# Top-k selection rounds moved from their own stage into VectorE's attention program

## The reference, cut to what matters

```python
def dsa_attention(q, k, v, iq, ik, iw, table):
    topk = min(TOPK_MAX, S // 4)                       # 128
    def block(args):                                   # one block of 128 queries
        logits = jnp.einsum('bqhd,bkd->bqhk', iqb, ik) * (IDX_DIM ** -0.5)
        score = jnp.einsum('bqhk,bqh->bqk', jax.nn.relu(logits), iwb)
        score = jnp.where(kpos <= qpos, score, NEG)
        _, idx = lax.top_k(score, topk)
        ...                                            # softmax over the 128 chosen keys alone
```

```python
        s = jnp.where(dist >= 0, s + bias[None, :, None], NEG)
        p = jax.nn.softmax(s, axis=-1)
        attn = p[:, :, 0] - lam * p[:, :, 1]
        return jnp.einsum('bhqk,bkhd->bqhd', attn, v32)
```

## Time and profile before

| | us |
|---|---|
| median of 3 runs (3939.85 to 3941.1) | 3940.17 |
| the profiled execution | 3943.98 |
| its span | 3942.2 |
| selection stage: first matmul to VectorE's last end | 3120.0 to 3187.9 |
| attention stage: first matmul to the last copy's end | 3189.5 to 3303.8 |

### The profile page before, as it was taken

The page is one execution under the profiler, slowest core; times in us unless marked ns, Lnnn a source line. Parts: engine busy times, 40 slices in busy tenths (PEclk is TensorE's granted clock), DMA queues, the critical chain, the costliest instruction groups (busy, mean ns, idle before and its releaser), DMA issues. The chain is left out here.

```text
span 3942.2 us, 48730 instructions
## 1 busy us (share of the span) xinstructions
PE 3447.4 (87%) x20802; PEld 2819.7 (72%) x20802; DVE 2049.6 (52%) x2787; ACT 1211.1 (31%) x1716; POOL 0.2 (0%) x4
## 2 busy tenths in 40 slices
PE   7999953688999999999944769999999957999998
PEld 6888842577688888888832668788888634868886
DVE  5444348646454445344357555453454487536565
ACT  3223222114332233223132024332232335434343
POOL 0000000000000000000000000000000000000000
PEclk9999977669999999999976569999999868999999
DMA  3322210003223222232200003122222110412222
GB/s 124 102 91 97 96 48 5 1 2 123 70 95 103 91 97 96 97 100 93 96 27 5 2 20 133 58 97 96 96 96 96 49 72 30 133 54 95 95 97 79
DMA packets 78095, 301.65 MB, mean 77 GB/s; under 512 B 8854, under 2 KB 9494, under 8 KB 77240
## 3 DMA queue, kind: packets, MB, share of 16 engines
q1 hardware_dynamic: 77880, 298.53, 22.4%
HBM read 292.47 MB, written 6.03 MB: 76 GB/s over the span
## 5 line engine op out<-in xcount | busy, mean ns | idle before, releaser
L307 DVE TENSOR_TENSOR w_lo<-ring,w_hi 128x1024 fp32r<-128x1024 f32 (+1 forms) x508 | 652.5, 1286 | 533.3 <-ACT w_hi L300 533.2
L319 PE MATMUL ps<-xa_hi,w_hi 128*128 128x512 f32 x1728 | 682.4, 395 | 83.9 <-DVE w_lo L307 82.4
L300 ACT ACTIVATE w_hi<-ring 128x1024 fp32r<-128x1024 f32 (+1 forms) x508 | 555.7, 1099 | 547.9 <-DMA ring<-in_mix_in_dram 203.0
L320 PE MATMUL ps<-xa_lo,w_hi 128*128 128x512 f32 x1728 | 676.6, 392 | 0.0
L321 PE MATMUL ps<-xa_hi,w_lo 128*128 128x512 f32 x1728 | 676.2, 391 | 0.0
L319 PE MATMUL ps<-xb_hi,w_hi 128*128 128x512 f32 x1248 | 487.9, 391 | 0.0
L321 PE MATMUL ps<-xb_hi,w_lo 128*128 128x512 f32 x1248 | 485.6, 389 | 0.0
L320 PE MATMUL ps<-xb_lo,w_hi 128*128 128x512 f32 x1248 | 485.6, 389 | 0.0
L319 PEld LDWEIGHTS ps<-xa_hi,w_hi 128*128 128x128 f32 x1728 | 326.5, 189 | 161.1 <-DVE w_lo L307 85.0
L320 PEld LDWEIGHTS ps<-xa_lo,w_hi 128*128 128x128 f32 x1728 | 327.0, 189 | 68.7 <-issue 1.9
L321 PEld LDWEIGHTS ps<-xa_hi,w_lo 128*128 128x128 f32 x1728 | 326.9, 189 | 68.5
(11 more groups left out here) (341 smaller groups left out, 3795.4 us busy)
## 6 DMA issues: line engine op xcount, KB each, us to landing
ring<-in_ffn_in_dram SPq DMA_DIRECT2D x176, 512.0 KB, 3.2
ring<-in_ffn_out_dram SPq DMA_DIRECT2D x64, 704.0 KB, 4.0
ring<-in_mix_in_dram SPq DMA_DIRECT2D x58, 512.0 KB, 3.2
ring<-in_up_dram SPq DMA_DIRECT2D x44, 512.0 KB, 3.2
ring<-in_w_in_dram SPq DMA_DIRECT2D x22, 512.0 KB, 3.2
ring<-in_down_dram SPq DMA_DIRECT2D x16, 704.0 KB, 4.1
ring<-in_mix_out_dram SPq DMA_DIRECT2D x16, 512.0 KB, 3.2
ring<-in_xk_dram SPq DMA_DIRECT2D x16, 512.0 KB, 3.3
```

What stands on the lines that cost most here:

```text
L300: act.activation(core.w_hi[j][:, 0:width], core.ring[j][:, 0:width], ACT.Copy).then_inc(self.halved, 1)
L307: dve.tensor_tensor(core.w_lo[j][:, 0:width], core.ring[j][:, 0:width], core.w_hi[j][:, 0:width].bitcast(F32), ALU.subtract).then_inc(self ...
L319: pe.matmul(out, hi, x_hi, start=(k == 0), stop=False)
L320: pe.matmul(out, hi, x_lo, start=False, stop=False)
```

## The change

The 16 rounds and the three last `tensor_scalar` leave the selection stage. In the attention stage VectorE runs one round (`choose(n)`) behind each of the units n = 0 to 15, and the three `tensor_scalar` behind unit 16. They now work in place, in `work`, which lies where `unpicked` lay. The sparse heads wait for them by a semaphore `chosen`.

```diff
-def select_keys_and_bias(core, rel_bias, reach_rows, reach_flags, skewed):
+def score_keys_and_bias(core, rel_bias, reach_rows, reach_flags, skewed):
...
-    work = core.scr[:, 5, :].rearrange("p (n k) -> p n k", n=3)
+    work = core.scr[:, 4, :].rearrange("p (n k) -> p n k", n=3)
...
-    unpicked = core.scr[:, 4, :].rearrange("p (n k) -> p n k", n=3)
-    best = core.small[:, 0:24].rearrange("p (n k) -> p n k", n=3)
...
-            maxed, out = [maxed0, maxed1, maxed2], [out0, out1, out2]
-            for n in range(TOPK // 8):
-                for i in range(1, QT):
-                    if n:
-                        dve.wait_ge(out[i - 1], n)
-                    dve.max(best[:, i - 1, :], work[:, i - 1, 0:(i + 1) * P]).then_inc(maxed[i - 1], 1)
-                for i in range(1, QT):
-                    row = work[:, i - 1, 0:(i + 1) * P]
-                    dve.wait_ge(maxed[i - 1], n + 1)
-                    dve.match_replace(row, best[:, i - 1, :], row, TAKEN).then_inc(out[i - 1], 1)
-            for i in range(1, QT):
-                dve.wait_ge(out[i - 1], TOPK // 8)
-                link(dve.tensor_scalar(unpicked[:, i - 1, 0:(i + 1) * P], work[:, i - 1, 0:(i + 1) * P], -2e38, NEG,
-                                       ALU.is_ge, ALU.mult))
...
@@ def block2_attention(core):
+    work = core.scr[:, 4, :].rearrange("p (n k) -> p n k", n=3)
+    best = core.small[:, 66:90].rearrange("p (n k) -> p n k", n=3)
...
                     if h >= 8 and i:
...
-                        dve.tensor_tensor(s, s, unpicked[:, i - 1, 0:width], ALU.add).then_inc(picked, 1)
+                        dve.wait_ge(chosen, 3)
+                        dve.tensor_tensor(s, s, work[:, i - 1, 0:width], ALU.add).then_inc(picked, 1)
...
+            maxed, out = [maxed0, maxed1, maxed2], [out0, out1, out2]
+
+            def choose(n):
+
+                for i in range(1, QT):
+                    if n:
+                        dve.wait_ge(out[i - 1], n)
+                    dve.max(best[:, i - 1, :], work[:, i - 1, 0:(i + 1) * P]).then_inc(maxed[i - 1], 1)
+                for i in range(1, QT):
+                    row = work[:, i - 1, 0:(i + 1) * P]
+                    dve.wait_ge(maxed[i - 1], n + 1)
+                    dve.match_replace(row, best[:, i - 1, :], row, TAKEN).then_inc(out[i - 1], 1)
...
             for n in range(len(units)):
                 turn_of(n + 2, n)
+                if n < TOPK // 8:
+                    choose(n)
+                if n == TOPK // 8:
+                    for i in range(1, QT):
+                        row = work[:, i - 1, 0:(i + 1) * P]
+                        dve.wait_ge(out[i - 1], n)
+                        dve.tensor_scalar(row, row, -2e38, NEG, ALU.is_ge, ALU.mult).then_inc(chosen, 1)
```

More of the change, by code:

```diff
@@ L1991, in select_keys_and_bias @@
     spread = core.spare[:, 0:HEADS * REACH].rearrange("p (h x) -> p h x", h=HEADS)
-    work = core.scr[:, 5, :].rearrange("p (n k) -> p n k", n=3)
+    work = core.scr[:, 4, :].rearrange("p (n k) -> p n k", n=3)
     part = core.scr[:, 6, 0:2 * S].rearrange("p (n k) -> p n k", n=2)
-    unpicked = core.scr[:, 4, :].rearrange("p (n k) -> p n k", n=3)
-    best = core.small[:, 0:24].rearrange("p (n k) -> p n k", n=3)
     n_parts = 3 * IDX
-    with stage(nc, "scored", "clipped", "added", "step", "maxed0", "maxed1", "maxed2", "out0", "out1", "out2",
+    with stage(nc, "scored", "clipped", "added", "step",
                "rows_in", "table_in", "flags_in", "made", "copied", "kept", "shifted") as (
-            block, scored, clipped, added, step, maxed0, maxed1, maxed2, out0, out1, out2,
+            block, scored, clipped, added, step,
             rows_in, table_in, flags_in, made, copied, kept, shifted):
@@ L2109, in block2_attention @@
     with stage(nc, "scored", "biased", "topped", "exped", "inverted", "shared", "turned", "turned_out", "gathered",
-               "stored", "weighted", "picked") as (
+               "stored", "weighted", "picked", "maxed0", "maxed1", "maxed2", "out0", "out1", "out2", "chosen") as (
             block, scored, biased, topped, exped, inverted, shared, turned, turned_out, gathered, stored,
-            weighted, picked):
+            weighted, picked, maxed0, maxed1, maxed2, out0, out1, out2, chosen):
         @block.tensor
@@ L2460, in block2 @@
     block2_small(core)
-    select_keys_and_bias(core, io["rel_bias"], io["reach"], io["flags"], skewed)
+    score_keys_and_bias(core, io["rel_bias"], io["reach"], io["flags"], skewed)
     block2_attention(core)
```

## The result

| kernel | median, us | runs, us | ratio to before, 95% interval |
|---|---|---|---|
| before, first comparison | 3940.64 | 3939.85 to 3943.39, n = 4 | |
| changed, first comparison | 4018.67 | 4016.93 to 4020.99, n = 4 | 1.0197 [1.0179, 1.0215] |
| changed, second comparison (29 runs of before) | 4019.27 | 4017.65 to 4023.47, n = 6 | 1.0123 [1.0071, 1.0175] |

The change costs 78 us in the first comparison, where 35.6 were forecast. The second ratio is smaller because the kernel before has two groups of times, which only the longer series of the experiments showed. In the three series behind the experiments 49 of its 89 runs took 3940 to 3949 us (the lower group) and 40 took 3981 to 3987 (the upper group), with nothing between. The runs that stand ahead of the prediction all fell in the lower group. All ten runs of the changed kernel lie at 4017 to 4023.

A forecast was written before the change was run, and what follows sets the result against it. VectorE was taken to bound heads 0 to 3, TensorE heads 4 to 11. Terms -6.1 + 44.4 - 1.7 - 1.0 + 0 = +35.6 us on 3940.2 gave 3975.8 us, range for 8 in 10 3967 to 3987.

The forecast's parts named there:

- What bounds what: Attention stage: VectorE bounds heads 0 to 3, TensorE bounds heads 4 to 11.
- The selection stage: Without the rounds, the bias read-back comes last, landing 11.0 us after issue; the stage gets 6.1 us shorter.
- Price and number of the rounds: Heads 0 to 3: rounds 0 to 14 are on the path, 15 x 2.96 = +44.4 us.
- the waits: Among the two-map units, VectorE's four waits for scores go: -1.7 us.
- round 15: Behind unit 15's combine: this round and the closing passes cost 0, barely covered by TensorE's work at 1.2 GHz.
- The backlog's -1.0: At unit 15: TensorE's backlog goes, so the transposes follow the combine some 0.1 us later: -1.0 us.
- TensorE's clock: Heads 4 and 5: low level again taken for 15 us, each microsecond at 1.2 GHz costing 0.40; its duration couldn't be read.
- rival 3: Heads 4 to 11: the clock stays low through all these single-map heads, +34 us, time 4010; chance 8%.
- Rival 1: Behind unit 15: the clock rises as soon as TensorE is dense, -3.6 us, time 3972; chance 20%.

The follow-up runs named there:

- e10: The changed kernel again, unaltered, beside more runs of before: 4017.65 to 4023.47 us, six of six.
- e3: Changed kernel with three added 128x128x512 matmuls in each of turns 15 and 16: 3981.4 to 3986.8 us, median 3983.5.
- e7: Kernel before with three added 128x128x512 matmuls in each of turns 15 and 16: 3941.1 to 3952.6 us, median 3949.3, ratio 0.9949.
- e1: Changed kernel with the 16 rounds left out of both stages: seven runs at 3933.2 to 3938.5 us, three at 3977.9 to 3982.3.
- e5: Changed kernel with rounds 0 to 7 in the selection stage, others behind units 0 to 7: four runs 3954.0 to 3958.5 us, six 3998.7 to 4002.9.
- e6: Changed kernel with rounds 0 to 7 in the selection stage, the others behind units 8 to 15: ten runs, 3983.6 to 4000.4 us.
- e9: Kernel before with one added matmul in each fourth unit of heads 4 to 11, eight in all: 3945.5 to 3959.9 us, median 3954.8.
- e2: Changed kernel with two added matmuls in each of turns 0 to 15: 3974.5, 3979.2, 4019.0 and 4019.5 us.
- e4: Changed kernel with rounds 0 to 13 back in the selection stage, 14 and 15 behind units 18 and 22, closing passes behind 23: median 3977.3 us.
- e8: As e4, with three added matmuls in each of turns 15 and 16: 3971.2 to 3983.0 us, median 3978.5.
- e12: Kernel before with two added matmuls in turns 1, 5, 9, 13 and one in 12, 14, 15: median 3940.8 us, ratio 0.9932.
- e13: As e12, plus two matmuls in turn 16, round 15 behind unit 15, closing passes behind 16: median 3937.6 us, ratio 0.9931 to before.

## Why the prediction was wrong

- **What bounds what** was right: VectorE in heads 0 to 3 (80.00 of 80 us busy in after, no wait for scores), TensorE in heads 4 to 11.
- **The selection stage** gave 6.9 us for the 6.1 forecast: the read-back landed in 10.7 for 11.0, and the way to it was a little shorter as well. In the second profile of the changed kernel (e10) it landed in 11.1, so this much varies from run to run.
- **Price and number of the rounds**: 42.0 us to the combine of unit 15 for 42.7 forecast, the waits were won back, and the transpose of unit 16 (3276.52) did not wait for round 15 at the low clock. The backlog's -1.0 came out too: unit 15's transposes follow its combine by 0.06 us, where it took 1.15 in before.
- **The sum of these** is confirmed a second way. Between the groups that can be compared, the changed kernel's 4019.0 is 35.7 us above before's upper group (median 3983.2), and e3 is 34.1 above e7, for 35.6 forecast.
- **The step that failed is TensorE's clock**: "How long the low level then lasts is what I can't read, and I take 15 us again." It lasted over all eight heads, which the prediction had as rival 3 at 8% and +34 us; measured +35.7 in the stretch behind unit 15, where -1.0 was forecast. The error was twofold. The prediction took the 15 us as a property of the heads, where it is one draw of a spread: 40 of 89 runs of the kernel before are 42 us slower. No profile of before fell on one of these; that they are low through these heads is inferred from their mean granted clock (0.897 to 0.902, against 0.909 to 0.913 in the lower group) and from e1's profile, whose heads 0 to 3 read as in before. The single execution that the prediction could read didn't show this. And it gave the sparse stretch ahead too little weight: by their times and granted clocks (0.892 to 0.895) all ten runs of the changed kernel have the long low stretch, and e5 and e6 point to the sparse units right ahead of head 4.
- **A size in rival 3 was off as well.** It took 12.25 us for a head at the low level. But within that head the clock had already risen in before:
```profile
3250.95 1.12 PE L2122 MATMUL ps<-big 64*128 64x512 f32 x2
```
Two scores of this form took 2.07 at the low level. A head that is low throughout takes 13.38, so a microsecond at the low level costs 0.45 and not 0.40, and the stretch came out 36.7 above its forecast, where rival 3 had 34.
- **Rival 1 fails**: by it the clock rises as soon as TensorE is dense. In the changed kernel it stayed at 0.50 through 95.00 busy us of 95. In before and e6 it rose under the same matmuls, after some 15 and 80 us, and with six or eight added matmuls no run's time shows the long low stretch (e3, e7, e9). So being back to back didn't settle the level here. What in TensorE's work kept it down was not separated: the scores contract over 64 rows, the gathers fill 64 columns, and transposes stand between them. In all six profiles that stayed low to the end (after, e1, e2, e4, e8, e10) the clock rose 3.5 to 9.1 us behind the last scores, with transposes and gathers still running, which speaks for the scores; in before and e6 it rose with scores still running, which speaks against them as the only cause. No kernel changed them alone. Nor do the runs show why before falls now in one group, now in the other.

## What to carry to other kernels

Work moved onto another engine's list can be priced within a microsecond or two from its rows and the total still be off by as much again, if it makes TensorE sparse ahead of a stretch that TensorE bounds. Read the granted clock there, and if TensorE is fully busy at 0.50 anywhere, count the whole stretch at either level and take more than one run before trusting a draw. Here a few added matmuls in TensorE's idle time ahead of such a stretch settled the level and cost next to nothing (e12, e13), while those on its own path cost 8 and 14 us (e7, e9). A stall of 1.56 us inside the stretch went with the loss of the level in e8.

## What the runs showed of the hardware that was not expected

- One kernel, two groups of times 42 us apart (medians 3941.5 and 3983.2), which goes with the granted clock of one stretch of about 100 us.
- Both levels hold for long on the same instructions: 95 us at 0.50 without an idle moment in the changed kernel, 54 us at 1.00 in e3. The high one was lost behind a stall of 1.56 us in e8 (where an equal one 9 us before had left it), and behind stalls of 0.87, 1.40 and 0.52 us in e2.
- VectorE's rounds beside the 3 MB read-back of the bias made no difference that shows: it took 10.7, 11.1, 11.0, 11.2 and 10.8 us in the profiles without them (after, e10, e1, e2, e3), 11.0 in before and 10.8 to 11.2 in the others.
